# Another order of the second stage's weight tiles in a two-layer mixer: convolution groups and pooling tiles first, four retention heads in a row

## The chip, the core and the metric

One core of a Trainium2 chip (trn2) runs the whole program. The metric is device time in microseconds (us). Five engines work side by side and meet through semaphores: TensorE (PE in the profile: matrix products), VectorE (DVE), ScalarE (ACT), GpSimd (POOL) and SyncE (SP, which starts most DMA transfers). The kernel before takes 2057.83 us, the median of three runs between 2057.62 and 2058.21.

## The reference, cut to what matters

The input is 512 positions of 1024 channels, the depth is two layers. In a layer the normed input is multiplied by one wide weight, `w_in`, and the columns of the product feed four branches; the branches are gated, merged, projected, and a feed-forward part follows.

```python
h = rms_norm(x, norm1_g)
z = h @ w_in
z_sc, z_q, z_kv, z_ng, z_ret, z_pool, z_gate = split(z)
y_a = b * causal_dwconv(c * h_, conv_w)        # z_sc -> b, c, h_ : three taps
y_b = nsa_mixer(z_q, z_kv, z_ng)               # attention, 8 heads, 3 kinds of keys
y_c = retention_mixer(z_ret)                   # 4 heads: rotary q and k, decay, norm, gate
y_d = pool_mixer(z_pool)                       # 4 groups: running means over 2, 4, 8, 16
merged = sum(einsum(branches, w_branch) * sigmoid(z_gate + b_gate))
x = x + merged @ w_o
x = x + (silu(causal_dwconv(u_gate)) * u_val) @ w_down
```

## The kernel before, in words

All activations lie transposed, channels on the 128 partitions and 512 positions along the row. A weight comes in groups of 8 blocks of 128x128 (512 KB). One group makes one tile of output, 128 channels by 512 positions. Each weight and each input is split in a high and a low part, so a block costs three products (lines 1220, 1221, 1222), a tile 24. The two accumulators `acc` in PSUM are used in turn: tile T can't start before VectorE has taken tile T-2 out (`take`, line 742: times `rstd`, into SBUF). ScalarE makes the high part of the group after next (`ahead`, line 459) once TensorE is through with a group, and GpSimd then makes the low part in two operations of about 1.3 us (line 437), both read from SBUF.

A layer has a first stage of 12 groups (keys, values, queries), a second stage of 32 tiles, and then the merge, `w_o`, the feed-forward parts. The change is in the second stage. It runs from about 84 to 372 us in the first layer and from 1099 to 1387 us in the second. Its 32 tiles are the inputs of four retention heads (`rq`, `rk`, `rv`, `rg`), of four convolution groups (`c`, `h`, `b`) and of four pooling groups (`u`). The table `B_TILES` gives their order. Each tile is run in four quarters of six products. After each quarter there is a slot, 128 in all, and `SIDE[slot]` lists the steps that are done there. Every engine goes through `SIDE` in the same order and does its own share of each step, so on VectorE, which takes a tile out after the fourth slot of the tile, a step that is late makes all behind it late.

The steps with a fixed place are those of attention: 22 visits, each with `scale`, `turn` (TensorE transposes into the banks `t`, VectorE copies them to `pT`, line 957), `values` (line 1435) and `scores` (line 1405, VectorE line 935, ScalarE's exponential line 571). Visits 14 to 21 stand in the slots 40 to 54, two slots apart. For each of the four blocks of queries there are also `cmp_scores`, `cmp_scale` and `cmp_turn`; the fourth block has them in slots 41, 43 and 45. There are two `t` banks and two `s` banks, each used in turn: a use waits until VectorE has freed the use before last.

The steps that the tables place are these. `conv` (four parts, lines 1032 to 1047) stands in the four slots after a tile `b`; its last part waits for ScalarE's copy of the third (line 597). After the take of an `h` tile VectorE multiplies it with `c` (line 1083). `mean` (four parts, lines 1057 to 1064) stands in the four slots after a tile `u`: each part adds the row to itself, shifted; the group with window 16 has four such sums, window 8 three, window 4 two, and the last part ends with lines 1063 and 1064. `rotate` stands two tiles after `rq` and `rk`. Its partner rows come by DMAs that ScalarE starts (lines 495, 496). A retention head's own steps start at `RET_SLOT`: scores and values in five slots (lines 1465, 1475), `ret_gate`, `ret_var`, `ret_inverse` (VectorE line 1001), `ret_spread` (TensorE line 1491), `ret_end`. Its transposed values are made by `ret_turn` (line 1456) in the slot after the tile `rg`. Before the change the heads start at slots 70, 80, 96 and 112.

Of the kernel before, what the change touches and what calls it, by code (L numbers as in the profile page):

```python
# [67 lines left out]


A_TILES = ["k_cmp", "v_cmp", "k_slc", "k_win", "v_slc", "v_win", "q0", "q1", "q2", "q3", "gate", "pad"]  # L70
RET0 = [0, 16, 20, 24]
SC0 = [4, 7, 10, 29]
RET_SLOT = [70, 80, 96, 112]
POOL0 = [28, 15, 14, 13]
POOL_SLOT = [127, 85, 101, 117]
B_TILES = [None] * B_GROUPS
for _h in range(RH):
    B_TILES[RET0[_h]:RET0[_h] + 4] = [("rq", _h), ("rk", _h), ("rv", _h), ("rg", _h)]
for _j in range(BC):
    B_TILES[SC0[_j]:SC0[_j] + 3] = [("c", _j), ("h", _j), ("b", _j)]  # L80
    B_TILES[POOL0[_j]] = ("u", _j)

# [29 lines left out]
for _h in range(RH):  # L112
    _n0 = RET_SLOT[_h]
    for _m in range(QT):
# [7 lines left out]
for _h in range(RH):  # L122
    SIDE[RET_SLOT[_h] + (9, 9, 9, 9)[_h]].append(("ret_end", _h))
    SIDE[RET_SLOT[_h] + (10, 10, 10, 11)[_h]].append(("ret_hi", _h))
    SIDE[RET_SLOT[_h] + (11, 11, 11, 13)[_h]].append(("ret_split", _h))
    SIDE[4 * (RET0[_h] + 3) + 3].append(("ret_turn", _h))
SIDE[2].append(("gate",))
# [1585 lines left out]
```

## Time and profile before

| what | us |
|---|---|
| median of the runs shown | 2057.83 |
| the profiled execution's own time | 2058.06 |
| its span, first to last instruction | 2056.3 |
| TensorE busy | 2032.3 (99%) |
| VectorE busy | 1162.2 (57%) |
| ScalarE busy | 679.3 (33%) |
| GpSimd busy | 918.6 (45%) |
| second stage of layer 1, 84 to 372: TensorE busy | 286.54 of 288 |
| the same for layer 2, 1099 to 1387 | 286.54 of 288 |

Two things help in reading it. First, busy TensorE time is modelled at its end: a product of 512 columns is shown with 0.39 us while the next starts 0.23 us after it. So an idle time of 0.68 that a row shows stands for a start that is later than the usual one by 0.16 more; the starts of two rows are the safer measure. Second, the shares of the whole span hide the stages: VectorE is busy for 57% of the span, but for 22.31 of the 28 us from 176 to 204.

### The profile page before, as it was taken

The page shows a single profiled execution, that of the slowest core. Times are in us where ns is not written, and L with a number is a line of the kernel's source. Part 1 is how long each engine was busy: PE and PEld are TensorE (multiplying, and loading weights), DVE is VectorE, ACT ScalarE, POOL GpSimd, SP SyncE. Part 2 cuts the span into 40 slices and gives each one's busy share as a digit, 9 for nine tenths or more (in the row PEclk, how much of TensorE's full clock was granted, in tenths as well). Part 3 has the DMA queues.
Part 4 walks back from the last instruction along what each step waited for, and adds up shares of the span by engine and source line. Part 5 has one row for each costly group of instructions (what it writes and reads, how often), then busy time and mean ns, then how long its engine had stood idle before and what let it go on. Part 6 is the DMA issues. An engine that isn't in the chain of part 4 may idle for free.

```text
span 2056.3 us, 31617 instructions
## 1 busy us (share of the span) xinstructions
PE 2032.3 (99%) x9916; PEld 1645.7 (80%) x9916; DVE 1162.2 (57%) x1709; ACT 679.3 (33%) x1011; POOL 918.6 (45%) x672
## 2 busy tenths in 40 slices
PE   8999999999999999999999999999999999999997
PEld 7777778888888888888887777778888888888886
DVE  7777755332327788862258667462232378888522
ACT  5366333333323222222234553333332332222222
POOL 4422233444445555555544223344444445555552
PEclk9999999999999999999999999999999999999999
DMA  5311232323222223223233112222222223223233
GB/s 212 108 53 42 77 94 81 102 92 102 92 96 98 92 92 102 92 96 112 93 128 96 52 42 90 91 87 98 96 98 93 100 82 103 100 94 102 96 105 109
DMA packets 57430, 194.88 MB, mean 95 GB/s; under 512 B 7040, under 2 KB 7552, under 8 KB 57216
## 3 DMA queue, kind: packets, MB, share of 16 engines
q1 hardware_dynamic: 52576, 186.17, 26.9%
q10 hardware_dynamic: 4768, 7.61, 1.5%
q8 instruction: 49, 0.80, 0.2%
q14 instruction: 37, 0.30, 0.0%
HBM read 186.67 MB, written 2.10 MB: 92 GB/s over the span
## 4 chain that ended last, share of the span: by engine, by line
PE 94%; DVE 3%; ACT 1%; issue 1%; DMA 0%; SPq 0%; ACTq 0%; DVEq 0%
PE acc L1220 28%; PE acc L1222 28%; PE acc L1221 28%; PE o L1435 2%; PE s L1405 2%; PE t L1416 2%; PE o L1475 1%; PE s L1465 1%; PE s L1313 0%; PE t L1456 0%; DMA w_raw<-weights_dram 0%; DVE sc L1058 0%; DVE pool_early L1064 0%; PE s L1501 0%; ACT pr_odd L571 0%
## 5 line engine op out<-in xcount | busy, mean ns | idle before, releaser
L437 POOL TENSOR_TENSOR w_lo<-w_raw,w_hi 128x512 fp32r<-128x512 f32 x668 | 918.4, 1396 | 1114.0 <-ACT w_hi L459 1097.7
L1220 PE MATMUL acc<-xg_hi,w_hi 128*128 128x512 f32 x1904 | 765.7, 402 | 6.9 <-DVE xg_lo L722 2.5
L1222 PE MATMUL acc<-xg_hi,w_lo 128*128 128x512 f32 x1904 | 743.0, 390 | 0.0
L1221 PE MATMUL acc<-xg_lo,w_hi 128*128 128x512 f32 x1904 | 742.1, 390 | 0.0
L459 ACT ACTIVATE w_hi<-w_raw 128x1024 fp32r<-128x1024 f32 x336 | 355.5, 1058 | 804.6 <-PE acc L1222 777.2
L1220 PEld LDWEIGHTS acc<-xg_hi,w_hi 128*128 128x128 f32 x1904 | 357.6, 188 | 111.1 <-issue 33.5
L1222 PEld LDWEIGHTS acc<-xg_hi,w_lo 128*128 128x128 f32 x1904 | 357.4, 188 | 76.0
L1221 PEld LDWEIGHTS acc<-xg_lo,w_hi 128*128 128x128 f32 x1904 | 358.0, 188 | 74.3 <-issue 3.8
L1097 DVE TENSOR_TENSOR work<-acc,rstd 128x512 f32<-128x512 f32 x64 | 44.1, 689 | 256.2 <-PE acc L1222 256.2
L1222 PE MATMUL acc<-act_hi,w_lo 128*128 128x512 f32 x352 | 137.0, 389 | 0.0
L1221 PE MATMUL acc<-act_lo,w_hi 128*128 128x512 f32 x352 | 137.0, 389 | 0.0
L1220 PE MATMUL acc<-act_hi,w_hi 128*128 128x512 f32 x352 | 137.0, 389 | 0.0
L1103 DVE SCALAR_TENSOR_TENSOR work<-work,acc 128x512 f32<-128x512 f32 x64 | 44.0, 687 | 103.1 <-PE acc L1222 103.1
L1191 DVE SCALAR_TENSOR_TENSOR x<-acc,x 128x512 f32 x16 | 11.1, 693 | 161.1 <-PE acc L1222 161.1
L1220 PE MATMUL acc<-y_hi,w_hi 128*128 128x512 f32 x256 | 99.6, 389 | 0.0
L1222 PE MATMUL acc<-y_hi,w_lo 128*128 128x512 f32 x256 | 99.6, 389 | 0.0
L1221 PE MATMUL acc<-y_lo,w_hi 128*128 128x512 f32 x256 | 99.6, 389 | 0.0
L645 ACT ACTIVATE work<-work 128x512 f32<-128x512 f32 x44 | 27.8, 632 | 192.2 <-DVE work L1146 192.2
L957 DVE COPY pT<-t 128x512 f32<-128x512 f32 (+1 forms) x88 | 52.5, 636 | 47.5 <-PE o L1435 47.1
L1220 PEld LDWEIGHTS acc<-act_hi,w_hi 128*128 128x128 f32 x352 | 66.1, 188 | 13.7
L1221 PEld LDWEIGHTS acc<-act_lo,w_hi 128*128 128x128 f32 x352 | 66.1, 188 | 13.7
L1222 PEld LDWEIGHTS acc<-act_hi,w_lo 128*128 128x128 f32 x352 | 66.1, 188 | 13.7
(209 smaller groups left out, 2187.3 us busy)
## 6 DMA issues: line engine op xcount, KB each, us to landing
w_raw<-weights_dram SPq DMA_DIRECT2D x339, 512.0 KB, 3.3
x<-xT_dram SPq DMA_DIRECT2D x8, 256.0 KB, 6.5
rot<-rq ACTq DMA_DIRECT2D x16, 128.0 KB
rot<-rk ACTq DMA_DIRECT2D x16, 128.0 KB
dec<-decay_dram ACTq DMA_DIRECT2D x8, 256.0 KB, 2.8
out_dram<-x SPq DMA_DIRECT2D x8, 256.0 KB, 2.7
con<-consts_dram SPq DMA_DIRECT2D x1, 1406.0 KB, 11.0
w1k<-w_dram SPq DMA_DIRECT2D x2, 512.0 KB, 8.8
```

The lines of the kernel that those rows point to most:

```text
L437: nc.gpsimd.tensor_tensor(w_lo[:, slot, part], w_raw[:, slot, part], w_hi[:, slot, part].bitcast(F32), ALU.subtract).then_inc(lo_ready, 1)
L459: nc.scalar.activation(w_hi[:, slot, :], w_raw[:, slot, :], ACT.Copy).then_inc(hi_ready, 1)
L645: nc.scalar.activation(work[:, 2, :], work[:, 1, :], ACT.Tanh, scale=0.5).then_inc(silu_ready, 1)
L957: t_end(ve.tensor_copy(pT[:, g, 0:w], t_of((*e, g))[:, 0:w]), (*e, g))
L1097: ve.tensor_tensor(work[:, n, :], acc[n % 2][:, :], rstd[:, :], ALU.mult).then_inc(acc_free, 1)
L1103: ve.scalar_tensor_tensor(out=work[:, n, :], in0=work[:, n, :], scalar=1.0, in1=acc[n % 2][:, :], op0=ALU.add, op1=ALU.mult).then_inc(acc_ ...
L1220: mm(tile, w_h, right_hi, start=first, stop=False)
L1221: mm(tile, w_h, right_lo, start=False, stop=False)
L1222: return mm(tile, w_l, right_hi, start=False, stop=last)
L1405: ins = mm(banks[g][:, i * w:(i + 1) * w], qT[r, j, qi * P:(qi + 1) * P], kT[r, br, 0:w], start=True, stop=True)
L1416: ins = nc.tensor.transpose(b[:, k * P:(k + 1) * P], pr_of(e[1], g)[:, k * P:(k + 1) * P], ident)
L1435: ins = mm(o_bank[qi % 2][d, j * P:(j + 1) * P], v[:, d], p[:, half, :], start=(br == 0 and k == 0 and (len(js) == 1 or i == 0)), stop=(br ...
```

## The change

Three convolution groups come first (tiles 0 to 8), then the pooling tiles of the windows 16, 8 and 4 (9 to 11), then the four heads in a row (12 to 27). The last four tiles stay. The first head's own steps start at slot 64 in place of 70, so that all heads stand 16 slots apart.

```diff
-RET0 = [0, 16, 20, 24]
-SC0 = [4, 7, 10, 29]
-RET_SLOT = [70, 80, 96, 112]
-POOL0 = [28, 15, 14, 13]
+RET0 = [12, 16, 20, 24]
+SC0 = [0, 3, 6, 29]
+RET_SLOT = [64, 80, 96, 112]
+POOL0 = [28, 11, 10, 9]
```

The order on VectorE in slots 4 to 12, before. `rk` and `rv_T` are takes of the head's tiles, lines 787 to 791 its rotation, `small` the factors of a visit.

```order
L742 TENSOR_TENSOR rk<-acc,rstd 128x512
L945 RECIPROCAL small<-small 128x8
L948 TENSOR_TENSOR small<-small,gates 128x8
...
L787 TENSOR_TENSOR rot<-rot,con 128x512
L789 TENSOR_TENSOR rq<-rq,con 128x512
L971 COPY cmp_pT<-t 128x256
L791 TENSOR_TENSOR rq<-rq,rot 128x512
L742 TENSOR_TENSOR rv_T<-acc,rstd 128x512
```

And now:

```order
L742 TENSOR_TENSOR sc<-acc,rstd 128x512
L1083 TENSOR_TENSOR sc<-sc 128x512
L945 RECIPROCAL small<-small 128x8
L948 TENSOR_TENSOR small<-small,gates 128x8
...
L971 COPY cmp_pT<-t 128x256
L742 TENSOR_TENSOR sc<-acc,rstd 128x512
```

The rotation has left this place, and the product of `h` and `c` has come in front of the factors of visit 0.

The order on VectorE in slots 43 to 45, before, from the end of `cmp_scale` to the copy of `cmp_turn` (line 971):

```order
L922 TENSOR_TENSOR cmp_p<-cmp_p,small 128x8x31
L1047 TENSOR_TENSOR y_lo_59<-sc,y_hi_55 128x512
L742 TENSOR_TENSOR sc<-acc,rstd 128x512
L945 RECIPROCAL small<-small 128x2
L948 TENSOR_TENSOR small<-small,gates 128x2
L957 COPY pT<-t 128x512
L957 COPY pT<-t 128x512
...
L971 COPY cmp_pT<-t 128x256
```

And now:

```order
L922 TENSOR_TENSOR cmp_p<-cmp_p,small 128x8x31
L1057 COPY sc<-sc 128x8
L1058 TENSOR_TENSOR sc<-sc 128x504
L1063 TENSOR_TENSOR sc<-sc,con 128x15
L1064 SCALAR_TENSOR_TENSOR pool_early<-sc 128x512
L742 TENSOR_TENSOR sc<-acc,rstd 128x512
...
L957 COPY pT<-t 128x512
...
L1057 COPY sc<-sc 128x1
L1058 TENSOR_TENSOR sc<-sc 128x511
L971 COPY cmp_pT<-t 128x256
```

The last part of a convolution has given place to the last part of the mean over 16, and the first part of the mean over 8 stands ahead of the copy.

On TensorE the only matrix product that changes its place within a layer, apart from head 0's own, is `ret_turn` of head 0: before, it stood behind `scores` of visit 3 (slot 15):

```order
L1405 MATMUL s<-kT,qT 128x256 x4
L1450 REGISTER_ALU
L1452 REGISTER_ALU
L1277 REGISTER_ALU
L1456 MATMUL t<-center,rv_T 128x128 x4
```

Now that slot ends with the scores, and the four products stand in slot 63, as those of the other heads stand in slots 79, 95 and 111:

```order
L1405 MATMUL s<-kT,qT 128x256 x4
L1232 REGISTER_ALU
L1233 REGISTER_ALU
L1220 MATMUL acc<-xg_hi,w_hi 128x512
L1221 MATMUL acc<-xg_lo,w_hi 128x512
```

## Rows read from the trace of the kernel before

**Rows 1.** The page's busy time: us, share of the span, number of instructions

```profile
PE 2032.3 (99%) x9916; PEld 1645.7 (80%) x9916; DVE 1162.2 (57%) x1709; ACT 679.3 (33%) x1011; POOL 918.6 (45%) x672
```

**Rows 2.** Waits of TensorE, whole span: total us, times, longest

```profile
PE acc L1220 <- DVE sc L742: 2.1, 4, 0.9
PE s L1394 <- DVE small L935: 1.4, 2, 0.7
PE s L1491 <- DVE small L1001: 1.2, 2, 0.6
```

**Rows 3.** Timeline of TensorE, second stage: start, us, line, operation, idle before

```profile
106.30 0.40 PE L1222 MATMUL acc<-xg_hi,w_lo 128*128 128x512 f32 x1
107.38 0.44 PE L1394 MATMUL s<-con,cmp_s 128*128 128x128 f32 x2 [0.68 <-DVE small L935]
...
247.64 0.39 PE L1222 MATMUL acc<-xg_hi,w_lo 128*128 128x512 f32 x1
248.19 0.47 PE L1220 MATMUL acc<-xg_hi,w_hi 128*128 128x512 f32 x1 [0.16 <-DVE sc L742]
...
268.69 0.39 PE L1222 MATMUL acc<-xg_hi,w_lo 128*128 128x512 f32 x1
269.70 0.65 PE L1491 MATMUL s<-con,small 128*128 128x128 f32 x4 [0.62 <-DVE small L1001]
```

**Rows 4.** Timeline of GpSimd, VectorE and ScalarE, slots 7 to 12

```profile
95.97 1.26 POOL L437 TENSOR_TENSOR w_lo<-w_raw,w_hi 128x512 fp32r<-128x512 f32 x1 [5.67 <-ACT w_hi L459]
98.47 0.22 DVE L948 TENSOR_TENSOR small<-small,gates 128x8 f32<-128x8 f32 x1
98.71 0.62 ACTq L496 DMA_DIRECT2D rot<-rk  x1
99.44 0.69 ACT L582 ACTIVATE pr<-pr,small 128x128 f32<-128x128 f32 x2 [3.55 <-DVE small L948]
105.02 0.20 DVE L945 RECIPROCAL small<-small 128x8 f32<-128x8 f32 x1 [0.23 <-ACT pr_odd L571]
```

**Rows 5.** Timeline of VectorE and GpSimd, mean over 16 in slots 56 to 59

```profile
230.50 0.14 DVE L1057 COPY sc<-sc 128x1 f32<-128x1 f32 x1
230.68 0.69 DVE L1058 TENSOR_TENSOR sc<-sc 128x511 f32<-128x511 f32 x1
...
236.83 1.39 POOL L437 TENSOR_TENSOR w_lo<-w_raw,w_hi 128x512 fp32r<-128x512 f32 x1 [6.21 <-ACT w_hi L459]
237.13 1.13 DVE L1063 TENSOR_TENSOR sc<-sc,con 128x15 f32<-128x15 f32 x1
238.29 1.74 DVE L1064 SCALAR_TENSOR_TENSOR pool_early<-sc 128x512 f32<-128x512 f32 x1
```

**Rows 6.** Timeline of VectorE, GpSimd and TensorE, slots 40 to 46

```profile
181.15 0.56 DVE L957 COPY pT<-t 128x384 f32<-128x384 f32 x1 [1.87 <-PE o L1435]
183.59 0.48 DVE L1032 TENSOR_SCALAR sc<-sc,vec 128x512 f32<-128x512 f32 x1
184.98 0.42 DVE L908 TENSOR_TENSOR cmp_p<-s,con 128x248 f32<-128x248 f32 x1
186.21 0.74 DVE L1035 SCALAR_TENSOR_TENSOR sc<-sc,vec 128x510 f32<-128x510 f32 x1
187.60 0.16 DVE L945 RECIPROCAL small<-small 128x2 f32<-128x2 f32 x1
191.02 0.42 DVE L922 TENSOR_TENSOR cmp_p<-cmp_p,small 128x248 f32<-128x248 f32 x1
192.53 0.69 DVE L742 TENSOR_TENSOR sc<-acc,rstd 128x512 f32<-128x512 f32 x1
192.71 2.53 POOL L437 TENSOR_TENSOR w_lo<-w_raw,w_hi 128x512 fp32r<-128x512 f32 x2 [10.60 <-ACT w_hi L459]
196.33 0.41 DVE L971 COPY cmp_pT<-t 128x256 f32<-128x256 f32 x1
196.88 1.04 PE L1416 MATMUL t<-con,pr_odd 128*128 128x128 f32 x8
```

## Prediction

> **What bounds the kernel.** I read the busy times first: TensorE works for 2032.3 us, 99% of the span [rows 1], and the change neither adds nor removes a matrix product. So the time can only move by what TensorE waits for inside the two second stages. The list of TensorE's waits comes next. Of its entries the reader should pick those whose line belongs to the second stage: once per layer it waits for the factors or scores of line 935, once for line 1001, and of the four waits for a take (line 742) two fall in this stage [rows 2]. Then the timeline gives each its true price, start to start, against the usual 0.23 us [rows 3]: 107.38 - 106.30 - 0.23 = 0.85 us in slot 13, 248.19 - 247.64 - 0.23 = 0.32 us at the tile of slot 64, and 269.70 - 268.69 - 0.23 = 0.78 us at `ret_spread` of head 0. All three are waits for VectorE. That is 1.95 us in a layer, 3.9 us in both: all that a better order can win here. What it can lose has no such bound, because VectorE works in one order and a late step holds all behind it. So the question for each place is how far VectorE is behind TensorE there, and whether the cover lasts.
>
> **What goes.** The wait at 269.70 is for `ret_inverse`, which in the old order stands behind the rotation of head 1's `rk`. With the head six slots earlier `ret_inverse` stands ahead of both rotations, as it does for the other three heads, and the wait list has this wait only once per layer [rows 2]: -0.78. The wait at 248.19 is for the take of a pooling tile; in slots 60 to 67 there is no mean any more, only rotation, one copy and head 0's scores: -0.32. The four products of `ret_turn` go from slot 15 to slot 63. They are the same four, alone in a slot rather than behind others; I take 0. Sum -1.10 us per layer.
>
> Head 0's rotation leaves slots 9 to 13 and its two DMA pairs, which ScalarE starts, move from tiles 1 and 2 to tiles 13 and 14. One start costs ScalarE up to 0.62 us [rows 4]. Queued behind them there are the factors of visits 19 and 21, which TensorE wants only a visit (about 6 us) later, so I cost them at nothing; if that cover were gone it would be about 1 us per layer.
>
> **Slots 7 to 13.** After the take of tile 1 VectorE now has the product of line 1083, the same kind as the 0.69 us sum of line 1058 [rows 5], ahead of the factors of visit 0. Before, the factors ended at 98.69 and yet ScalarE began to scale only at 99.44, because it was starting the DMAs of `rk` until 99.33 [rows 4]. These are gone. So 0.7 us more on VectorE is met by 0.7 us less on ScalarE, and the exponentials that VectorE waits for at 105.02 [rows 4] would come when they came. By this the wait of 0.85 us in slot 13 stays as it is, since the chain to it goes through 105.02 and not through the rotation that was removed: +0, and not the gain that the removal suggests. Against it stands GpSimd: its first operation began at 95.97 and the second follows it, to about 98.6, and line 1083 would begin at about 98.15 with both inputs in SBUF. In the one place where rows show long VectorE operations beside GpSimd, they were late [rows 5]; that gives up to +0.5. I take +0.5, since a small product at 98.47 also took 0.22 us [rows 4], and keep 0 and 0.7 as ends.
>
> Here the Trainium skill has a rule ("SBUF — State Buffer", section "SBUF: two separate sides"): the port pair that VectorE and GpSimd share is an exclusive lock, and a VectorE operation with two SBUF inputs waits for the whole of a GpSimd operation that reads SBUF. By it the sum has the +0.5 here, without it 0. The rows of the mean over 16 agree with it (1.13 us for 15 columns); of line 1083 beside GpSimd no row here shows it.
>
> **Slots 40 to 46, where the new order costs.** Before, convolution group 1 stood in slots 40 to 43. Its parts took 184.98 - 183.59 = 1.39 us, 187.60 - 186.21 = 1.39 us, and the last, from the end of `cmp_scale` at about 191.36 to the take at 192.53, 1.17 us: 3.95 us [rows 6]. Now the mean over 16 stands there. A part is 0.90 us (0.18 to the sum, 0.69, and a gap of 0.03) [rows 5]; four of them are 3.6 us. The last part has also lines 1063 and 1064, which took 1.13 and 1.74 us, with the gap before the take 3.0 us [rows 5]. Sum 6.6 us, 2.65 us more. Is the 3.0 right here too? The operation of 15 columns can't need 1.13 us of itself, and a GpSimd pair had begun 0.3 us before it [rows 5]. In slots 43 to 44 a pair began at 192.71, after a copy of ScalarE that the new order hasn't got there [rows 6]; so it will begin near 192, when VectorE, 1 us late after three parts of a mean in place of two of the convolution, comes to these very lines. I take the full 3.0; without the meeting it would be about 1.0.
>
> The first part of the mean over 8 stands ahead of the copy of `cmp_turn` (line 971): +0.90. And at the beginning, VectorE now comes to slot 40 from a convolution (group 2, slots 36 to 39) whose last part waits for ScalarE; it had 1.87 us of idle time before 181.15 [rows 6], which covers most of it: +0.3, between 0 and 0.6. Together the copy of line 971 ends 2.65 + 0.9 + 0.3 = 3.85 us later than the 196.74 of before: at 200.6. From 181.15 on VectorE had no idle time left to give but 0.28 us, and all transfers between it and ScalarE are counted in the spacings.
>
> TensorE needs that copy. With two `t` banks the second half of `turn` of visit 15 (slot 46), which began at 196.88 + 0.52 = 197.4 [rows 6], waits until `cmp_turn` is copied; and `cmp_turn` itself waits for the first copy of visit 14. So the cover was 0.66 us and the new stall is 200.6 - 197.4 = 3.2 us, split between slots 45 and 46. Once TensorE has waited, VectorE is no longer behind; the means over 8 and 4 have one and two sums less, while TensorE's tiles grow with the visits, so they don't build a new lag. Ends: 1.2 us when GpSimd doesn't meet lines 1063 and 1064, 3.7 us when line 1058 is caught too and VectorE comes 0.6 late.
>
> **Other places.** Convolution group 1 is now in slots 24 to 27 with `cmp_scores` and `cmp_scale` of the third block: 3.95 us more than before on VectorE, 0.7 less for a product of line 1083, over some 12 us. By the same count VectorE comes to slot 28 about 2 us late and has hardly 0.5 us of cover at slots 29 and 30. I cost it at nothing; if that cover is gone, up to 1 us per layer.
>
> **Sum.** Per layer -1.10 + 0.5 + 3.2 = +2.6 us, in two layers +5.2 us. The profiled execution took 2058.06 us itself, 0.2 above the median; from the median 2057.83 + 5.2 = 2063.0 us. So: slower, by 0.25%. What can be told from no change in this kernel is about 0.2%, 4.1 us.
>
> **Rivals.**
>
> *The meeting with GpSimd doesn't happen.* Both the +0.5 and 2.0 of the 3.2 us are gone: -1.10 + 1.2 = +0.1 per layer, 2058.0 us. For it: GpSimd's start hangs on ScalarE, which also shifts, and in slots 56 to 59 VectorE met it because it was late. Against it: VectorE is as late in the new place, and the pair lasts 2.5 us.
>
> *VectorE's slack swallows the means, and the cleaner places of head 0 are what is left.* This is the case on the other side. Its mechanism is at slot 46: if the copy of line 971 ends before 197.4 + the shift of TensorE, only -1.10 per layer is left, 2055.6 us; if the wait in slot 13 goes too (the rotation is no longer in front), -1.95 and 2053.9 us. It decides at 0.66 us: a lag of VectorE below that costs nothing. For it: 1.87 us of idle time at 181.15. Against it: that idle time lies before the stretch, not in it, and the pure operation time of the added parts, without GpSimd, is already +1.5 us.
>
> *The lag is larger.* The tight place at slots 28 to 30 also stops TensorE (up to 1 us), and the stall at 46 has its upper end (3.7): +4.1 per layer, 2066.0 us.
>
> **Chances.** The forecast (2061.5 to 2064.5) 0.50, the first rival 0.27, the one on the other side 0.11, the larger lag 0.12. The range that holds it 8 times in 10 reaches from the first rival to the last: 2057.2 to 2066.2. Slower by over 0.2% (above 2061.95) is most of the forecast's part and all of the larger lag: 0.56. Within 0.2%: 0.40. Faster by over 0.2% needs 4.1 us, more than all the waits of this stage together: 0.04.
>
> **What would show it.** In the new trace `ret_spread` of head 0 has no wait and neither has the tile of slot 64. In slots 45 and 46 TensorE's transposes (lines 1446 and 1416) have idle time before them with VectorE as its end, some 3 us in both, in each layer. Lines 1063 and 1064 of the first mean take about 1.1 and 1.7 us. The wait before line 1394 in slot 13 is 0.7 to 1.2 us. The forecast is wrong if the transposes of slots 45 and 46 follow their neighbours in 0.23 us, or if TensorE waits in another slot for more than 1 us.

## The result and the profile after

The changed kernel takes 2063.81 us (median of 11 runs, 2063.41 to 2064.76); the kernel before, timed with it, 2058.20 us. The ratio is 1.0027 with a 95% interval of 1.0019 to 1.0034: slower by 5.6 us. The profiled execution has a span of 2062.0 us, 5.7 more than the one of before. The starts of the same products in the two traces say where the 5.7 lie: 2.7 us in the second stage of layer 1, 3.8 in that of layer 2, and 0.9 the other way in the first 10 us of the program, which the change doesn't touch. One execution of the last experiment took 8887 us at a granted clock of 0.22 and is left out of account; all others lie below 2068 us.

The new list of TensorE's waits (engine, line, what for: total us, times, longest) answers to [rows 2]:

```profile
PE t L1446 <- DVE pT L957: 4.3, 2, 2.2
...
PE s L1394 <- DVE small L935: 2.0, 2, 1.0
PE acc L1220 <- DVE sc L742: 1.8, 2, 0.9
...
PE t L1416 <- DVE cmp_pT L971: 1.0, 1, 1.0
...
PE s L1383 <- DVE gates L890: 0.5, 1, 0.5
```

Line 1491 (`ret_spread`) has gone from the list, and of the four waits for a take the two of this stage have. The wait of line 1394 has grown. The first row is new: `cmp_turn` in slot 45 waits 2.15 us in each layer. The last row, a wait for the gates in slot 3 of layer 2, is new as well; it comes up again at the end.

The timeline of TensorE in slots 45 and 46 of layer 1 (start, us, line, operation, idle before), which answers to the last of [rows 6]:

```profile
193.85 0.40 PE L1222 MATMUL acc<-xg_hi,w_lo 128*128 128x512 f32 x1
196.40 0.44 PE L1446 MATMUL t<-con,cmp_p 128*128 128x128 f32 x2 [2.15 <-DVE pT L957]
...
198.07 0.60 PE L1416 MATMUL t<-con,pr_odd 128*128 128x128 f32 x4
199.63 0.65 PE L1416 MATMUL t<-con,pr_odd 128*128 128x128 f32 x4 [0.96 <-DVE cmp_pT L971]
```

Start to start the first wait costs 196.40 - 193.85 - 0.23 = 2.32 us, and the second, where four transposes usually take about 0.5 us, 1.05 us. Together 3.4 us. Measured by the products behind slot 46, which in this layer fall back against the old trace, it is 3.5 us.

VectorE in slots 43 to 45 and GpSimd beside it:

```profile
190.09 0.42 DVE L922 TENSOR_TENSOR cmp_p<-cmp_p,small 128x248 f32<-128x248 f32 x1
190.43 1.24 DVE L1057 COPY sc<-sc 128x8 f32<-128x8 f32 x1
191.70 1.70 DVE L1058 TENSOR_TENSOR sc<-sc 128x504 f32<-128x504 f32 x1
193.43 0.17 DVE L1063 TENSOR_TENSOR sc<-sc,con 128x15 f32<-128x15 f32 x1
193.64 0.69 DVE L1064 SCALAR_TENSOR_TENSOR pool_early<-sc 128x512 f32<-128x512 f32 x1
194.46 0.69 DVE L742 TENSOR_TENSOR sc<-acc,rstd 128x512 f32<-128x512 f32 x1
...
195.65 1.29 DVE L957 COPY pT<-t 128x512 f32<-128x512 f32 x2
...
199.15 0.42 DVE L971 COPY cmp_pT<-t 128x256 f32<-128x256 f32 x1 [0.20 <-DVE sc L1058]
```

```profile
190.24 2.61 POOL L437 TENSOR_TENSOR w_lo<-w_raw,w_hi 128x512 fp32r<-128x512 f32 x2 [8.79 <-ACT w_hi L459]
```

GpSimd's pair of subtractions began at 190.24, while the last operation of `cmp_scale` (190.09) was running, and so the two operations that were late beside it are the copy of 8 columns and the last sum (1.24 and 1.70 us, usually 0.17 and 0.69), not lines 1063 and 1064 as in [rows 5]. The sum of the delays is 2.1 us; there it was 2.0. TensorE's first wait ends with the first of the two copies at 195.65, its second with the copy at 199.15.

In slots 7 to 13 the product of line 1083 stands where it was expected: at 97.27 in a layer in which TensorE is 0.88 us ahead of the old trace, so at 98.15 on the old scale. GpSimd's pair runs beside its first part (95.10 to 97.79). ScalarE begins to scale at 98.90, 99.78 on the old scale and so 0.34 later than in [rows 4]. TensorE's wait, which answers to the first pair of [rows 3], is now 1.01 in place of 0.68 us:

```profile
97.27 1.07 DVE L1083 TENSOR_TENSOR sc<-sc 128x512 f32<-128x512 f32 x1
98.46 0.20 DVE L945 RECIPROCAL small<-small 128x8 f32<-128x8 f32 x1
```

```profile
98.90 2.46 ACT L582 ACTIVATE pr<-pr,small 128x128 f32<-128x128 f32 x8 [3.88 <-DVE small L948]
```

```profile
106.83 0.44 PE L1394 MATMUL s<-con,cmp_s 128*128 128x128 f32 x2 [1.01 <-DVE small L935]
```

### The profile page after: what moved, and what is told of

Read it like the earlier page. It is cut to its first block, busy times and chain, and to the rows that moved or that the text cites. A ratio compares the mean times of both kernels' runs of the same rounds, so it can differ in the third digit from the quotient of the medians.

```text
span 2062.0 us, 31613 instructions
## 1 busy us (share of the span) xinstructions
PE 2035.1 (99%) x9916; PEld 1647.6 (80%) x9916; DVE 1162.6 (56%) x1709; ACT 678.9 (33%) x1011; POOL 918.9 (45%) x672
## 4 chain that ended last, share of the span: by engine, by line
PE 92%; DVE 4%; issue 2%; ACT 1%; DMA 0%; SPq 0%; DVEq 0%; ACTq 0%
PE acc L1220 28%; PE acc L1222 28%; PE acc L1221 28%; PE o L1435 2%; PE s L1405 1%; PE t L1416 1%; PE o L1475 1%; PE s L1465 1%; DVE sc L1058 0%; PE s L1313 0%; PE t L1456 0%; DVE sc L742 0%; DVE pr L935 0%; PE s L1501 0%; DMA w_raw<-weights_dram 0%
## 5 line engine op out<-in xcount | busy, mean ns | idle before, releaser
L459 ACT ACTIVATE w_hi<-w_raw 128x1024 fp32r<-128x1024 f32 x336 | 355.2, 1057 | 807.6 <-PE acc L1222 780.9
```

The lines of the kernel that those rows point to most:

```text
L459: nc.scalar.activation(w_hi[:, slot, :], w_raw[:, slot, :], ACT.Copy).then_inc(hi_ready, 1)
```

## The experiments

All times are medians. Each kernel was timed over 11 runs, the first (e1) over 5; the kernel before had 2058.4 us beside e1 to e4 and 2058.65 beside the last three. "Stage" is the time from the first product of the gate (line 1370) to the last pooling products (line 1501) in the profile, layer 1: 275.3 us before, 278.0 after. It shows a change of a few tenths better than the medians do, because the changed kernel's trace has 1.1 us in layer 2 (the gates 0.6, a lower clock 0.5; see the end) that most of the experiments' traces don't have there.

**e1, head 0's steps at slot 70 again**

```diff
-RET_SLOT = [64, 80, 96, 112]
+RET_SLOT = [70, 80, 96, 112]
```

> The changed kernel with one number put back: head 0's own steps start at slot 70 again, while its tiles stay at 12 to 15. My theory: `ret_inverse` of head 0 again stands behind the rotation of head 1's `rk`, so the wait of `ret_spread` (0.78 us start to start before) comes back in each layer: 2063.8 + 1.6 = 2065.4 us, and the other waits stay. Rival (the old wait came from the means in front of it, slots 56 to 67, and not from the rotation): no wait comes back, 2063.8 us.

Measured: 2065.64 us (ratio to before 1.0035, 1.0022 to 1.0049), 1.8 us above the changed kernel. The wait is back at its old size, with no mean anywhere near:

```profile
PE s L1491 <- DVE small L1001: 1.3, 2, 0.6
```

So this wait belonged to the rotation in front of `ret_inverse`. By the products on both sides of head 0's steps the six slots are worth 0.87 us in layer 1 and 0.83 in layer 2. The stage of layer 1 is longer by 1.6 us, since 0.7 more went in slot 46, where TensorE's clock fell in this trace (see the end).

**e2, the small means first**

```diff
-POOL0 = [28, 11, 10, 9]
+POOL0 = [28, 9, 10, 11]
```

> The changed kernel with the pooling tiles in the order of windows 4, 8, 16 in place of 16, 8, 4. Slots 40 to 43 then hold two sums in place of four. My theory (VectorE is late at the copy of line 971, by the added sums and by the meeting with GpSimd): the slots lose 1.8 us of sums, and lines 1063 and 1064 come before GpSimd's pair begins, about 1.9 us more; that is more than the 3.3 us stall, so the stall in slots 45 and 46 is gone: 2063.8 - 6.6 = 2057.2 us. Rival (GpSimd plays no part, only the sums count): -1.8 us per layer, 2060.2 us. Second rival (the stall just moves to slots 48 to 51, where the mean over 16 now is): no gain, 2063.8 us.

Measured: 2056.33 us (0.9991, 0.9982 to 1.0000); stage 274.5 us. Waits for lines 957 and 971 are gone from the list, and nothing has come in slots 48 to 51. VectorE ends the mean as the pair begins:

```profile
189.96 0.15 DVE L1063 TENSOR_TENSOR sc<-sc,con 128x3 f32<-128x3 f32 x1
190.14 0.69 DVE L1064 SCALAR_TENSOR_TENSOR pool_early<-sc 128x512 f32<-128x512 f32 x1
190.95 0.69 DVE L742 TENSOR_TENSOR sc<-acc,rstd 128x512 f32<-128x512 f32 x1
...
195.69 0.42 DVE L971 COPY cmp_pT<-t 128x256 f32<-128x256 f32 x1 [0.20 <-DVE sc L1058]
```

```profile
190.79 2.50 POOL L437 TENSOR_TENSOR w_lo<-w_raw,w_hi 128x512 fp32r<-128x512 f32 x2 [8.79 <-ACT w_hi L459]
```

The two waits were worth 3.6 us a layer here by the products behind them. The same tiles in the same slots, only two of the three exchanged, give 7.5 us back. Both rivals fall: more went than the sums alone (1.8 us a layer), and nothing moved to a later slot. How much of it is GpSimd, e2 can't say, since the sums go with it; that is e3's question.

**e3, GpSimd's pair later**

```diff
-                    ahead(L, A_GROUPS + b)
+                    if b != 11:
+                        ahead(L, A_GROUPS + b)
...
+                        if n == 44:
+                            ahead(L, A_GROUPS + b)
```

> The changed kernel, but ScalarE makes the high part of the group after tile 11's in slot 44 behind its other steps and not ahead of them, so GpSimd's pair begins some 8 us later and not beside the last part of the mean over 16. Nothing is taken away. My theory (exclusive use by GpSimd of what VectorE needs costs the last part 2.0 us): VectorE is 2.0 us less late, the stall falls from 3.3 to 1.3 us per layer, 2063.8 - 4.0 = 2059.8 us, and lines 1057 and 1058 take 0.17 and 0.69 us in slot 43. Rival (the long times are VectorE's own): same rows, same 2063.8 us. Second rival (the weights then come late): TensorE waits for w_lo, slower than 2063.8.

Measured: 2058.93 us (1.0005, 0.9996 to 1.0014), 4.9 us less than the changed kernel; stage 275.8. VectorE's lines, three numbers higher here, in slot 43:

```profile
191.28 0.17 DVE L1060 COPY sc<-sc 128x8 f32<-128x8 f32 x1
191.47 0.68 DVE L1061 TENSOR_TENSOR sc<-sc 128x504 f32<-128x504 f32 x1
192.19 0.17 DVE L1066 TENSOR_TENSOR sc<-sc,con 128x15 f32<-128x15 f32 x1
192.40 0.69 DVE L1067 SCALAR_TENSOR_TENSOR pool_early<-sc 128x512 f32<-128x512 f32 x1
```

```profile
198.89 2.60 POOL L437 TENSOR_TENSOR w_lo<-w_raw,w_hi 128x512 fp32r<-128x512 f32 x2 [16.58 <-ACT w_hi L459]
```

VectorE does exactly what it did, and the same operations take 0.17 and 0.68 us when GpSimd isn't at work. On TensorE the wait before `cmp_turn` has shrunk from 2.32 to 0.21 us, and the 0.95 us before the second half of `turn` has stayed:

```profile
PE t L1419 <- DVE cmp_pT L974: 1.9, 2, 1.0
```

So 2.1 us per layer go with the meeting with GpSimd. That makes 4.2 of the 4.9 us; in layer 2 this trace has neither the wait for the gates nor the lower clock of the changed kernel's.

**e4, `cmp_turn` two slots later**

```diff
-        SIDE[_at + 4].append(("cmp_turn", _qi))
+        SIDE[_at + (6 if _qi == 3 else 4)].append(("cmp_turn", _qi))
```

> The changed kernel with `cmp_turn` of the fourth block in slot 47 in place of 45; its result is first used in slot 48. VectorE's work stays the same. My theory (the stall is the turn-taking of the two t banks: `cmp_turn` waits for the first copy of visit 14, and `turn` of visit 15 for the copy of `cmp_turn`): what is left is `turn` of visit 15 waiting for its own factors, about 0.6 us in place of 3.3: 2063.8 - 5.4 = 2058.4 us. Rival (TensorE waits for VectorE in general, whatever bank): the wait moves to `turn` of visit 15 at its full size, 2063.8 us.

Measured: 2061.87 us (1.0019, 1.0010 to 1.0028), 1.9 us less than the changed kernel and not 5.4. The list shows why:

```profile
PE t L1416 <- ACT pr_odd L582: 2.0, 2, 1.0
PE t L1416 <- DVE cmp_pT L971: 1.8, 2, 0.9
...
PE t L1446 <- DVE pT L957: 0.4, 2, 0.2
```

`turn` of visit 15 now waits 1.0 us for its own factors, which VectorE makes late and ScalarE after it, and a visit later the second half of `turn` waits for the copy of line 971 again. There is even a third wait, of 0.2 us, before `cmp_turn`. The theory that the banks' turn-taking is the stall was wrong as a whole: it decides at which instruction TensorE meets a late VectorE. Moving the meeting gives what VectorE makes up meanwhile, and that is little: the stage of layer 1 is 277.6 us, 0.4 less. The median shows more (1.0 us a layer), but in layer 2 this trace again has neither the wait for the gates nor the lower clock, so not all of that is the move's.

**f3, the first part of the next mean behind the copy**

```diff
-            SIDE[4 * (_b + 1) + _k].append(("mean", B_TILES[_b][1], _k))
+            SIDE[4 * (_b + 1) + (1 if _k == 0 and B_TILES[_b][1] == 2 else _k)].append(("mean", B_TILES[_b][1], _k))
```

> The changed kernel (windows 16, 8, 4) with the first part of the mean over 8 done in slot 45 behind the copy of line 971, in place of slot 44 ahead of it. VectorE's work stays the same. My theory (this part was 0.9 us of the stall): the copy comes 0.9 to 1.1 us sooner, the wait of 1.1 us before the second half of `turn` of visit 15 goes, the one before `cmp_turn` (2.3 us) stays: 2063.8 - 2.0 = 2061.8 us. Rival (only the first wait matters, the second is a leftover of it that comes back elsewhere): 2063.8 us.

Measured: 2062.27 us (1.0018, 1.0008 to 1.0027), 1.5 us less. The second wait is gone, the first is as it was:

```profile
196.49 0.44 PE L1446 MATMUL t<-con,cmp_p 128*128 128x128 f32 x2 [2.15 <-DVE pT L957]
198.16 1.14 PE L1416 MATMUL t<-con,pr_odd 128*128 128x128 f32 x8
```

```profile
198.16 0.42 DVE L971 COPY cmp_pT<-t 128x256 f32<-128x256 f32 x1
```

The stage is shorter by 1.0 us, as the theory had it; the median gives 1.5 for both layers where 2.0 were expected. So e3 takes away the first wait and leaves the second, f3 the other way round: the second is the 0.9 us part of a mean that stood ahead of the copy. A kernel with both edits wasn't run.

**f1, the `cmp` steps of the second block one slot later (on e2's order)**

```diff
-        _at = _n + 1
+        _at = _n + (2 if _qi == 1 else 1)
```

> The order with the small means first, and the three `cmp` steps of the second block one slot later (14, 16, 18 in place of 13, 15, 17). My theory: the wait of 1.17 us in slot 13 is for VectorE to free the s bank that `scores` of visit 2 used in the slot before; with one more quarter of a tile (1.4 us) in between it is covered, -1.17 us per layer, 2056.3 - 2.3 = 2054.0 us. Rival (TensorE is only held there because VectorE is late in general, and waits one slot later instead): 2056.3 us.

Measured: 2058.16 us (1.0000, 0.9991 to 1.0009), 1.8 us slower than e2. The wait in slot 13 is gone. There are a small new one, 0.29 us before `scores` (line 1405) in slot 15, and a large one, 1.46 us, in slot 18: `cmp_scale` now stands behind the visit's copies and scores, the last part of the convolution and a take, and TensorE comes to `cmp_turn` first:

```profile
PE t L1446 <- DVE cmp_p L922: 2.9, 2, 1.5
```

As in e4, a step that was moved away from a late VectorE found it late elsewhere.

**f2, the product of line 1083 in slot 9 (on e2's order)**

```diff
+                        if n == 9:
+                            then(ve.tensor_tensor(sc[:, 1, :], sc[:, 1, :], sc[:, 0, :], ALU.mult))
...
-                    if kind == "h":
+                    if kind == "h" and b != 1:
```

> The order with the small means first, and the product of line 1083 for tile 1 done in slot 9, behind the scores of visit 1, in place of right after the take of tile 1. My theory: the chain to the wait in slot 13 starts with the factors of visit 0, which stand behind this product (1.19 us with GpSimd's part); without it ScalarE scales 1.15 us sooner and the wait of 1.17 us shrinks to nothing: 2056.3 - 2.3 = 2054.0 us. If only GpSimd's 0.38 us of it counted: 2055.6 us. Rival (the chain is set by something else, such as the scaling of visit 0 on ScalarE alone): no change, 2056.3 us.

Measured: 2054.74 us (0.9981, 0.9972 to 0.9990), the fastest of all, 3.9 us below the kernel before and 9.1 below the changed one. The wait list has no entry of slot 13 any more; ScalarE's scaling began right behind the factors:

```profile
98.48 0.22 DVE L948 TENSOR_TENSOR small<-small,gates 128x8 f32<-128x8 f32 x1
```

```profile
98.73 2.46 ACT L582 ACTIVATE pr<-pr,small 128x128 f32<-128x128 f32 x8 [2.83 <-DVE small L948]
```

On TensorE the transpose of line 1394 (two numbers higher here) follows without a wait:

```profile
106.30 0.40 PE L1224 MATMUL acc<-xg_hi,w_lo 128*128 128x512 f32 x1
106.67 0.44 PE L1396 MATMUL s<-con,cmp_s 128*128 128x128 f32 x2
```

The factors ended at the same point as before the change (98.70), and ScalarE started 0.03 us later, not 0.75 as in [rows 4], with the DMA starts gone. Against the kernel before, TensorE gains 0.70 us at this place.

## Why the prediction was right, point by point

The forecast was 2063.0 us with a chance of 0.56 for slower. Its steps, per layer:

| step | predicted us | measured us |
|---|---|---|
| `ret_spread` of head 0 | -0.78 | gone; 0.87 and 0.83 come back in e1 |
| tile of slot 64 | -0.32 | gone, -0.40 |
| values of head 0 in slot 71 | 0 | -0.26 |
| `ret_turn` moved | 0 | TensorE 0.91 us earlier after slot 15, 0.88 later after slot 63 |
| wait in slot 13 | +0.5 | +0.34 |
| slots 45 and 46 | +3.2 | +3.5 |
| `cmp_turn` of the second block | 0 | +0.30 |
| all | +2.6 | +2.7 |

The measured numbers are those of layer 1: how much more a place sets the same products back, or lets them come sooner, than in the old trace. The first three rows are read from e1's trace, in which head 0's steps stand in their old slots. The mechanism was right. That the time came out so near is in part chance. The terms were off by up to 0.3 us, some 0.6 in sum on either side, and nearly cancel. And the two stages cost 6.5 us in the trace, not 5.2: layer 2 has 1.1 us that the prediction didn't foresee, while the start of the program gave back 0.9.

*Slots 45 and 46.* The sum was right in size, and e3 and f3 take it apart: 2.1 us go with GpSimd's pair (predicted 2.0), 1.0 with the part of a mean ahead of the copy (predicted 0.9), the rest is the added sums less the cover. The copy ended at 199.57 in a layer in which TensorE was 1.18 us ahead of the old trace, so at 200.75 on the old scale, where 200.6 was predicted.

That the meeting with the pair came about as forecast was luck in its timing. The prediction had VectorE 1 us late after three parts of a mean. Its own numbers give 0.2 (2.7 us for three parts against 2.78 for two of the convolution, and 0.3 from the slots before), and the trace 0.25. It had the pair near 192; on the old scale it began at 191.4. The two errors went the same way, so the pair met VectorE all the same, one sum earlier: lines 1057 and 1058, not 1063 and 1064. The price hardly changed, since VectorE had SBUF work ready at either place. The +0.3 at the beginning wasn't there (the scores of line 935 in slot 40 began at 182.36 on the old scale, as before), and the four parts with their gaps took 7.05 us, 5.0 without the pair's 2.1, where 6.6 was predicted with it.

*The rule of the Trainium skill* ("SBUF — State Buffer", "SBUF: two separate sides") held for the operations with two inputs in SBUF: in slot 7 the product took 1.07 us beside GpSimd, 0.38 more than alone, and in slot 43 the sum of line 1058 took 1.70 in place of 0.69. The copy of line 1057 has a single input and was late too (1.24 in place of 0.17), which the rule as the prediction tells it doesn't cover. e3, which only moved the pair in time, takes both back to 0.17 and 0.68 us. So it is shown that GpSimd's work beside them makes them late; that a lock is the means is not something a run here can show.

*Slot 13.* The step that the gain of the rotation would be eaten up by the product was right, and f2 shows the other half: without the product in front, the wait of before goes too. The +0.5 was 0.16 too much. The price of the old wait was also set too high. The prediction took 0.23 us as the usual distance, which holds between two products, but in f2 line 1394 starts 0.37 us behind the last product without any wait. So the 0.85 was 0.71, which is what f2 gives back (0.70), and the idle time of 0.68 in [rows 3] was nearly the whole price.

*Tight places.* Slots 28 to 30, costed at nothing, cost nothing: TensorE's distance to the old trace is 1.18 us from slot 21 to slot 44. Head 0's DMA starts in tiles 13 and 14 cost nothing either; the distance doesn't change from slot 47 to slot 62. Not foreseen was slot 18, where the second half of a `turn` waited 0.30 us for the copy of `cmp_turn`; it is the same mechanism as in slot 46, behind the last part of convolution group 0. The wait list doesn't show it; a group of eight transposes took 1.33 us in place of 1.03. Nor does it show the 0.26 us that head 0's values waited in slot 71 of the old order.

*The rivals.* That the meeting with GpSimd doesn't happen, with a chance of 0.27, did not come about. e3 is that case made by hand for slot 43 alone: 2058.9 us, where the prediction had 2058.0 with the 1.0 us of slot 13 gone as well. The larger lag (0.12) didn't come either: slots 28 to 30 held, though the stall came near its upper end of 3.7. The one on the other side (0.11) needed a lag of less than 0.66 us, and VectorE's was 4. It is what e2 brings about: 2056.3 us, where the rival said 2055.6. The bound of 3.9 us on any gain was reached by f2 and not passed.

In layer 2 the stage took 279.0 us in the profile, 3.8 more than before. 0.6 of that is a wait for the gates in slot 3 and 0.5 a lower clock of TensorE in slots 45 and 46; both are described below.

## What to carry to other kernels

When the busiest engine waits for nothing, an order of work can gain only the few waits in the list, but can lose what the second engine's slack no longer covers; so count the second engine's work between two meetings, not over the stage. Into that count belongs what its operations take beside GpSimd's, not alone: up to the copy of line 971 the new order made VectorE 4.0 us later, 1.9 by work and gaps and 2.1 by the pair. And a step that is moved to a later slot (e4, f1) helps little or not at all when its maker is late; taking work out from in front of it (e2, f2, f3) does.

## What the runs showed of the hardware

A copy of 8 columns within SBUF took 1.24 us and a product of 15 columns 1.13 us [rows 5] beside GpSimd's subtraction, 0.17 us each without it. A reciprocal of 8 columns took 0.20 us beside the pair (at 98.23 in the trace of before, the pair from 95.97 to 98.66) and the same 0.20 behind it (98.46 above). Copies from PSUM weren't slowed: those of line 957 took 0.54 to 0.69 us, whether GpSimd was at work when they began (36 of them in the trace of before) or not (52). Which operation is hit depends on where the pair begins. A pair cost VectorE 2.0 us in [rows 5] and 2.1 in slot 43, where such work stood ready all along. In slot 7, where a take lay between, it cost 1.4 us: 0.38 in the product and 1.0 in line 922, which took 1.44 in place of 0.42 us before and after the change alike.

Layer 2 of the changed kernel shows only one wait in slots 45 and 46, and the time is lost all the same. The windows before, during and after the transposes (busy us and counts of the engines, then TensorE's granted clock) show it:

```profile
1212.00:1216.00 4.00, 1.85 (x10) 1.25 (x9) 3.63 (x9) 1.58 (x3) 0.00 (x0) 1.00 0.38 131
1216.00:1219.50 3.50, 3.50 (x15) 2.40 (x15) 3.11 (x10) 1.76 (x5) 0.00 (x0) 0.52 0.00 0
1219.50:1224.00 4.50, 4.50 (x32) 3.13 (x32) 4.03 (x12) 2.81 (x7) 0.00 (x0) 1.00 0.01 4
```

TensorE stood idle for 2.15 us, worked again for 1.0 us at the full clock, and was then granted 0.52 from 1216 to 1219.5, in effect the lower level of 1.2 GHz. Its products came 0.42 us apart in place of 0.23:

```profile
1216.12 0.63 PE L1220 MATMUL acc<-xg_hi,w_hi 128*128 128x512 f32 x1
1216.55 0.63 PE L1221 MATMUL acc<-xg_lo,w_hi 128*128 128x512 f32 x1
```

In layer 1 the same idle time was followed by a clock of 1.00, in e1 it was layer 1 that fell (0.71 in the window 197.5 to 201) and not layer 2, and in f3, with the same idle time in both layers, neither fell. So of six such waits two were followed by a fall. It partly hid behind the wait for line 971 that was to come anyway: slots 45 and 46 together set TensorE back by 4.0 us against the old trace, 3.5 in layer 1. It stays open what decides it.

The wait for the gates (0.54 us, slot 3 of layer 2) is another meeting with GpSimd, on work of the first stage, which the change doesn't touch: VectorE's line 882, just ahead of the gates, took 1.42 us there and 0.28 in the trace of before. e2's trace has it too, the other seven don't. With one trace of each kernel nothing here shows whether it belongs to the kernel or to the execution.
